# Mix stage of a hybrid decoder layer: levels in two halves, another place for the memory probabilities, VectorE's edges and denominators moved

## What the kernel computes

```python
x += 0.5 * swiglu_1(rmsnorm(x))
h = rmsnorm(x); P = h @ W_in                        # columns split per group
# A: sliding-window attention: 8 query heads, 2 key heads, window 128, sinks, T5 bias
# B: gated linear attention, 4 heads with 32 key and 64 value columns:
#      b = cumsum(log_a);  A[i, j] = sum_d q[i,d] k[j,d] exp(b[i,d] - b[j,d]),  j <= i
#      o = A @ v + (q * exp(b)) @ S;   S' = exp(b_last) * S + (k * exp(b_last - b))^T @ v
# C: cross-attention, 4 heads, into 256 memory tokens: softmax(q k^T / 8) @ v
x += concat(A, B, C) @ W_out
x += 0.5 * swiglu_2(rmsnorm(x))
```

## Time and profile before

| | us |
|---|---|
| median of 3 runs (lowest, highest) | 1718.3 (1718.25, 1718.56) |
| the profiled execution | 1718.25 |
| its span, first to last instruction | 1716.5 |
| TensorE busy | 1698.9 (99%) |
| VectorE busy | 1124.1 (65%) |
| ScalarE busy | 718.2 (42%) |
| GpSimd busy | 531.5 (31%) |

### The profile page before, as it was taken

How to read it: one execution, slowest core, us unless ns; L and a number is a source line. 1 busy time by engine, 2 the same in 40 slices (tenths; PEclk the granted TensorE clock), 3 DMA queues, 4 the chain that set the end, 5 groups by cost and what they waited for, 6 DMA issues and landing times.

```text
span 1716.5 us, 24866 instructions
## 1 busy us (share of the span) xinstructions
PE 1698.9 (99%) x8329; PEld 1385.5 (81%) x8329; DVE 1124.1 (65%) x1575; ACT 718.2 (42%) x1350; POOL 531.5 (31%) x432
## 2 busy tenths in 40 slices
PE   9999999999999999999989999999999999999999
PEld 6788888888888889887766688888888888888887
DVE  7975555555498596347888863985555555569654
ACT  5533333333344563232177832543333333334442
POOL 0454445544130141000056612145554444310000
PEclk9999999999999999999999999999999999999999
DMA  7342222233774431120100122222233322485434
GB/s 207 72 151 92 98 98 92 104 117 121 271 245 125 157 98 68 50 85 25 37 2 2 38 99 99 74 99 92 92 110 121 111 104 92 171 282 160 136 103 166
DMA packets 101694, 191.71 MB, mean 112 GB/s; under 512 B 11491, under 2 KB 13972, under 8 KB 101612
## 3 DMA queue, kind: packets, MB, share of 16 engines
q1 hardware_dynamic: 100528, 188.48, 32.4%
q0 software_dynamic: 848, 2.10, 0.9%
q10 hardware_dynamic: 236, 0.06, 0.0%
HBM read 139.74 MB, written 50.86 MB: 111 GB/s over the span
## 4 chain that ended last, share of the span: by engine, by line
PE 92%; DVE 3%; ACT 1%; POOL 1%; issue 1%; DVEq 0%; ACTq 0%
PE ps L56 29%; PE ps L57 29%; PE ps L58 29%; PE ps L1675 1%; PE ps L1603 1%; PE ps L1307 1%; ACT glu L1808 1%; POOL Pg L1975 1%; DVE loT L373 1%; PE ps L1593 1%; PE ps L1724 0%; DVE ring L502 0%; PE ps L1712 0%; PE ps L1398 0%; PE ps L1698 0%
## 5 line engine op out<-in xcount | busy, mean ns | idle before, releaser
L502 DVE TENSOR_TENSOR ring<-w_raw,ring 128x512 fp32r<-128x512 f32 x240 | 239.9, 1015 | 219.0 <-ACT ring L497 218.9
L56 PE MATMUL ps<-hiT,ring 128*128 128x512 f32 x672 | 261.5, 389 | 1.5 <-DVE ring L502 1.5
L58 PE MATMUL ps<-hiT,ring 128*128 128x512 f32 x672 | 261.5, 389 | 0.0
L57 PE MATMUL ps<-loT,ring 128*128 128x512 f32 x640 | 249.0, 389 | 0.0
L56 PE MATMUL ps<-down_ring 128*128 128x512 f32 x616 | 239.7, 389 | 0.0
L57 PE MATMUL ps<-down_ring 128*128 128x512 f32 x616 | 239.6, 389 | 0.0
L58 PE MATMUL ps<-down_ring 128*128 128x512 f32 x616 | 239.6, 389 | 0.0
L56 PE MATMUL ps<-hiB,ring 128*128 128x512 f32 x576 | 224.9, 390 | 0.0
L58 PE MATMUL ps<-hiB,ring 128*128 128x512 f32 x576 | 224.1, 389 | 0.0
L497 ACT ACTIVATE ring<-w_raw 128x512 fp32r<-128x512 f32 x240 | 150.4, 628 | 165.4 <-PE ps L58 164.0
L876 ACT ACTIVATE down_ring<-down_raw 128x512 fp32r<-128x512 f32 x176 | 109.1, 630 | 226.0 <-DMA down_raw<-act_dram 184.2
(11 more groups left out here) (259 smaller groups left out, 3004.1 us busy)
## 6 DMA issues: line engine op xcount, KB each, us to landing
down_raw<-act_dram SPq DMA_DIRECT2D x154, 256.0 KB, 2.6
w_raw<-in_w_gate SPq DMA_DIRECT2D x88, 256.0 KB, 3.0
w_raw<-in_w_up SPq DMA_DIRECT2D x88, 256.0 KB, 3.1
act_dram<-actT SPq DMA_DIRECT2D x88, 256.0 KB, 2.0
act_dram<-act SPq DMA_DIRECT2D x66, 256.0 KB, 2.0
wd<-in_w_down SPq DMA_DIRECT2D x44, 256.0 KB, 4.9
wd_mirrored<-in_w_down SPq DMA_DIRECT2D x33, 256.0 KB, 4.6
p_raw<-in_w_proj SPq DMA_DIRECT2D x15, 512.0 KB, 3.6
```

The source lines that it names most:

```text
L56: nc.tensor.matmul(out, w_hi, x_hi, start=first, stop=False, skip_group_check=resumed)
L57: nc.tensor.matmul(out, w_hi, x_lo, start=False, stop=False, skip_group_check=resumed)
L58: return nc.tensor.matmul(out, w_lo, x_hi, start=False, stop=last, skip_group_check=resumed)
L502: nc.vector.tensor_tensor(ring[:, e % RING, 1, :], op_source(e), ring[:, e % RING, 0, :].bitcast(F32), ALU.subtract).then_inc(op_ready, 1)
```

## The change

Four edits. Levels are issued in two calls, of heads 0 and 1 ahead of TensorE's waits for swa_lo, mem_lo and the copy of the output, and of heads 2 and 3 behind them. The transposed probabilities of unit 2 go to rstd, over those from which they were made, and the waits for the reader go from pt_copy(0) and pt_copy(2) to mem_exps. gate_edges of the next block runs ahead of update_state, instead of at the head of that block. denominators(0) of the next block run behind gate_q instead of behind mem_lo.

```diff
@@ -161,7 +161,7 @@
         A_T = (A_T0, A_T1)
         bias, Pg0 = place(184 * KB, ("bias", [P, SWA_HEADS, 2 * P], F32), ("Pg0", [P, 4, 2 * P], F32))
         P_of = [Pg0[:], Pg1[:], rstd[:].rearrange("p (h k) -> p h k", h=4)]
-        PT = (glu, PT1, glu)
+        PT = (glu, PT1, rstd[:].rearrange("p (t q) -> p t q", t=2))
 
         ps = ctx.enter_context(nc.psum_tensor("ps", [P, 8, HALF], F32))
         BANK_X, BANK_Y, BANK_BIAS, BANK_WARM, BANK_NORM = (0, 2), (1, 3), 4, 5, 6
@@ -1651,16 +1651,20 @@
                 pe.wait_ge(q_gated, n + 1)
                 pe.wait_ge(k_gated, n + 1)
                 wait(pe, pt_ready, unit_count(2, n - 1))
+                head_levels(n, (0, 1))
                 wait(pe, swa_lo_ready, n)
                 wait(pe, mem_y_lo_ready, n)
                 wait(pe, o_copied, n)
+                head_levels(n, (2, 3)).then_inc(level_ready, 1)
+
+            def head_levels(n, heads):
                 for l in range(SPLITS):
                     c = P >> (l + 1)
-                    for h in range(GLA_HEADS):
+                    for h in heads:
                         r = slice(h * GLA_DK, (h + 1) * GLA_DK)
                         to = ps[:, LEVEL_BANK + h, l * HEAD:(l + 1) * HEAD].rearrange("p (a c) -> p a c", c=c)
                         mm = nc.tensor.matmul(to, kg_of(n)[r, l, :], upper(qg[n % 2][r, l, :], l), start=True, stop=True)
-                mm.then_inc(level_ready, 1)
+                return mm
 
             def turn(u, n):
                 pe.wait_ge(scaled, scaled_count(u, n))
@@ -1788,7 +1792,7 @@
 
             def mem_exps(n):
                 act.wait_ge(shifted, 5 * n + 5)
-                wait(act, turned, unit_count(2, n - 1))
+                wait(act, values_done, unit_count(2, n - 1))
                 for i in range(4):
                     c = 8 + i
                     nc.scalar.activation(P_of[2][:, i, :], ps[:, SCORE_BANK[2] + i // 2, (i % 2) * MEM:(i % 2 + 1) * MEM],
@@ -1797,12 +1801,8 @@
 
             def pt_copy(u, n):
                 act.wait_ge(turned, unit_count(u, n))
-                if u == 0:
-                    wait(act, values_done, unit_count(2, n - 1))
-                elif u == 1:
-                    wait(act, values_done, unit_count(1, n - 1))
-                else:
-                    act.wait_ge(values_done, unit_count(0, n))
+                if u < 2:
+                    wait(act, values_done, unit_count(u, n - 1))
                 tiles = key_tiles(n, u)
                 at = slice(tiles[0], 2)
                 nc.scalar.activation(PT[u][:, at, :], ps[:, TURN_BANK[u] + tiles[0]:TURN_BANK[u] + 2, :], ACT.Copy
@@ -1927,8 +1927,6 @@
             mem_max(0)
             for n in range(NB):
                 more = n + 1 < NB
-                if n:
-                    gate_edges(dve, n)
                 if not more:
                     gate_out(n - 1)
                 denominators(dve, 1, n)
@@ -1939,8 +1937,10 @@
                 if more:
                     if n:
                         gate_out(n - 1)
+                    gate_edges(dve, n + 1)
                     update_state(n)
                     gate_q(n + 1)
+                    denominators(dve, 0, n + 1)
                     bias_max(dve, 1, n + 1)
                 else:
                     unit_vector(dve, NPROJ)
@@ -1949,7 +1949,6 @@
                 swa_lo(n)
                 mem_lo(n)
                 if more:
-                    denominators(dve, 0, n + 1)
                     mem_max(n + 1)
 
         def mix_pool(pool):
```

## The result

| | before | after |
|---|---|---|
| median of 4 runs each (lowest, highest), us | 1718.4 (1718.3, 1720.1) | 1731.9 (1730.4, 1735.1) |
| the profiled execution, its span | 1718.25, 1716.5 | 1730.41, 1728.6 |

The ratio is 1.0072, with a 95% interval of [1.0059, 1.0084]: slower. These medians differ by 13.5 us; the kernel before, run again beside the experiments, had medians of 1719.0 to 1720.2, and against those the loss is 12 to 13 us, as the ratio has it. Forecast were 1727.2 and a range of 1721.5 to 1731.5; the median lies 0.4 us above that range.

The account below looks back on a forecast made before the run. TensorE, busy 99% of the span, was taken to bound the kernel. First block 1.5, six intervals of 1.11 (6.7) and last block 0.7 gave 8.9 us on 1718.25, so 1727.2 as median; range 1721.5 to 1731.5.

Parts of the forecast that it names:

- (a): Mix-stage levels in two halves: 28 rounds of weight loads instead of 14, 1.57 us more TensorE work in each block.
- V: Mark in each mix-stage block: the start of mem_values; from it to S 7.55 us were forecast, where 6.63 stood.
- S: Mark in each mix-stage block: the start of the spans; from it to the next V 8.85 us were forecast.
- (b): Mem probabilities in their own place: TensorE's 0.32 us wait ahead of mem_values goes in each block.
- (c): gate_edges ahead of update_state: they meet GpSimd's scale(2), which releases turn(2); 0.20 us taken, bounds 0 and 0.39.
- turn(2)'s wait: Sign to look for in the mix-stage blocks: turn(2) on TensorE waits 0.3 to 0.5 us for GpSimd.
- (d): denominators(0) ahead of bias_max(1) on VectorE: delay of bias_max(1) between 0 and 0.28 us, taken as 0.
- the port case: row_sum held behind gate_q until GpSimd's gate_k ends: some 1.6 us a block, about 1728; considered within the 7% rival.
- TensorE's work alone: Rival, 15%: TensorE's work sets the mix stage's pace, all idle time used up, 0.71 us more a block: 1724.6.
- The exchange of gate_q: Rival, 10%: scale(2) slides, VectorE's gate_q reads first and turn(2) waits for both, some 0.9 us more a block: 1732.6.
- Cheap halves: Rival, 7%: the levels' two halves cost what the whole did, 2.8 us less in all: 1715.5.
- nothing: Rival, 6%: nothing measurable, as part of the levels' rounds overlaps and the rest is paid by (b) and (d): 1718.

## Why the prediction was right, and where its size was off

**The direction and the levels, (a): right.** Forecast were 3.1 to 3.4 us; measured 3.16 to 3.21, in 28 rounds, and some 4.9 at the full clock when there are 56. The Trainium skill ("TensorE: Matmul & The Clock Gate", LDWEIGHTS) gives the time of a load as its columns / 1.2, 107 ns for 128 columns; the 0.09 to 0.13 us a round are near that, though one load's record lasts 187 ns. The start of the levels came at V+2.08 (forecast 2.1), S in the clean block at V+7.58 (forecast 7.55). Part of this is luck: the levels were 0.15 shorter, and scores(0) then waited 0.24 for ScalarE's mem_exps. One sentence of (a) failed: "The second half's waits are then long met." Where they are, the levels take 2.96. Timelines of VectorE, first in the changed kernel, then in the one with the halves alone:

```profile
935.00 0.41 DVE L1922 TENSOR_TENSOR hT_lo<-ps,hT_hi 128x256 fp32r<-128x256 f32 x1
```

```profile
929.87 0.42 DVE L1926 TENSOR_TENSOR hT_lo<-ps,hT_hi 128x256 fp32r<-128x256 f32 x1 [0.30 <-ACT hT_hi L1841]
```

With the halves alone, mem_lo ends at 930.29, ahead of the levels (930.40). In the changed kernel it ends at 935.41, 1.32 us behind the start of the levels (934.09) and just ahead of the second half. Two halves kept apart by a wait take 1.78 each (986.50), 3.56 together: so at 2.96 the second half's first rounds run beside the last ones of the first, and at 3.2 less of them does. That the late mem_lo is the reason fits these times; no run tried it alone.

**The own place, (b): right, and worth more.** From the second block on, no mem_values waits for ScalarE any more (the first still does, 0.77). I paid it 0.32, the idle time shown. Alone, it shortens S to V from 8.64 to 8.12, by 0.52: from values(1) to mem_values it is 0.90 us without a wait (0.86 in the changed kernel) and was 1.35 with it, of which 0.32 was idle. The other 0.13 is overlap: values(1) takes 1.03, and without a wait mem_values starts 0.13 before its end.

**The edges, (c): right.** scale(2) was to grow by 0.20 from 1.93; it measures 2.17 in the clean block. Where the clock had fallen, the edges came late (927.36) and turn(2) had no wait at all (946.18). The prediction names that as the sign that its size is wrong.

**turn(2)'s wait: right in the clean block alone.** Forecast 0.3 to 0.5, measured 0.36 at 979.36, S+5.72 (forecast 5.87). S to V is then 8.52, not 8.85: 0.15 from the shorter levels and 0.18 from (b)'s overlap. So a clean block is 16.10 and not 16.40, 0.83 more than before and not 1.11.

**denominators(0), (d): wrong.** "I take 0" was the step. I had priced the two instructions at their own 0.28 and held the port case, 2.1 a block, to cost nothing as bias_max(1) had time. The runs show that row_sum can take 0.74 to 2.05, that TensorE was 2.38 us idle behind the longest without the halves, and 0.33 and 0.52 between the halves in the changed kernel; by the ratios the move costs about 5 us of the change. It was seen as a mechanism, under a rival, and thrown out of the sum. The Trainium skill ("SBUF — State Buffer", Who interferes with whom) says that a VectorE instruction with two SBUF inputs contends with a GpSimd one that reads SBUF. The 2.04 to gate_k's end and the 0.75 to set_diagonal's agree, while the 0.15 right behind gate_q in other blocks has no gate_k left to meet (929.13 + 2.10 is past by 932.10).

**The clock: missing.** No step had it, as the mix stage before had 1.00 throughout. Five of the six intervals between the V marks hold a fall. Such a block is 0.92 longer than the clean one (17.02 less 16.10): about the 1.60 of slower matmuls less the 0.61 of idle time that they use up. The sum redone from V to V: 6 x 0.83 = 5.0 for the mechanics, 5 x 0.92 = 4.6 for the clock, and 0.66 more in the first of them (17.69), behind the row_sum of 2.04 (0.33 of idle time between the halves, and no overlap of the two): 10.2 of 10.26. The first stretch was forecast at 1.5 and measured 1.44, which is luck in part, as it holds a fall (869.6) that the forecast didn't have; the last was forecast at 0.7 and measured 1.86, with the fall at 989.1 and a row_sum of 2.05 in it. For the mix stage the forecast was low by 4.7 us (13.57 less 8.9), which is 4.6 for the clock and 1.8 in the two stretches with a long row_sum (the last has a fall too), less 1.7 by which it was too high in the mechanics of the six blocks. Without that last error it would have been further off.

**The rivals.** TensorE's work alone: not so in the clean block (0.61 idle), but so with the low clock, where all of 17.02 us is busy. The exchange of gate_q: it came in another form, GpSimd's gate_k ahead of VectorE's gate_q. Cheap halves and nothing: out, by the levels' length.

**Open:** what makes the clock fall in one execution of a kernel and not in another. The traces show that in the mix stage it falls within the levels or at most 1.3 us behind them, that ten of the twelve traces have a fall in the first block, even those of the two kernels that are as fast as before, that kernels with long levels have more of it (five to eight times in the mix stage, one of them only twice), and that one kernel with short levels, the place alone, can be in either way. They don't show which change of order would prevent it, nor which part of a disturbed block's exchange feeds the next fall.

## What to carry to other kernels

Small matmuls that sit in different rows of the array paid by the round here, so don't split their turn-taking to start some of them early: here 0.14 us of early start cost 1.2 of rounds. Price a short two-input instruction on VectorE, before you move it, at the end of what GpSimd is reading then, not at its own length. And in a stretch where TensorE is nearly full, look at the granted clock of several executions before trusting a gain of half a microsecond a block: what the clean block shows and what the median shows can have opposite signs (the place alone: 14.8 to 15.0 against 15.3 a block, and 1725.2 against 1719.5 in all).

## What the hardware showed unasked

- One program, two times: the place alone gave 1716 to 1722 us or 1728 to 1733 us, with a mean granted clock of 0.996 to 0.999 in the one group and 0.991 to 0.993 in the other; in the trace of the slower one the clock falls in seven blocks in a row.
- Two engines that read the same places exchange their order by a small shift: gate_q and gate_k take 1.6 and 2.95 us, or 2.6 and 2.1. In kernels where they don't meet they take 1.08 and 2.09, but there gate_q meets set_diagonal, which takes 1.9 instead of 1.04.
- Removing a wait of 0.32 us ahead of a matmul gave 0.45 at that place, since its start then overlaps the end of the one before.
- A round of weight loads also goes by the granted clock: head by head, where each record is a round of its own, one took 0.087 us at 1.00 and 0.17 at 0.50.
